# Opening the normed phases of a two-layer streaming encoder with two weight slabs at once

## The reference, cut to what matters

```python
h = rmsnorm(x, norm_mix[0]); proj = h @ l0_w_in          # u, v, z, xbc, dt
ya = gmlp_mix(u, v, ...)
yb = rmsnorm(y_ssd * silu(z), ssm_norm)                  # n_yb
x = x + concat([ya, yb]) @ l0_w_out                      # outa (ya), outb (yb)
for i in (0, 1):
    if i == 1:
        h = rmsnorm(x, norm_mix[1])                      # n_mix1
        x = x + retention_mix(h, ...)                    # heads_a, ret_a, heads_b, ret_b
    h = rmsnorm(x, norm_ffn[i])                          # n_ffn0, n_ffn1
    x = x + (silu(causal_dwconv(h @ w_gate)) * (h @ w_up)) @ w_down   # gu, down
    gate = sigmoid(rmsnorm(x, norm_ple[i]) @ ple_w_gate[i])           # n_ple
    x = x + gate * (p[i] @ ple_w_proj[i])                             # gate, pp
y = rmsnorm(x, norm_final)                               # n_out
```

## The kernel before, in words

| join | last phase | normed phase | norm | slabs after the norm are read by |
|---|---|---|---|---|
| A | z | outb | n_yb | DVE `scaled`, add to x (L1671) |
| B | outb | gu00 | n_ffn0 | gate slab: `scaled`, conv taps (L1697, L1707, L1709 twice), SiLU on ACT, times rstd on POOL (L604); up slab: DVE L1717, L1718 |
| C | gate0 | heads_a | n_mix1 | k and q slab: `scaled`, times cos (L1344), halves swapped by ACT, times sin on POOL (L588), sum (L1347) |
| D | ret_b | gu10 | n_ffn1 | as B |

## Time and profile before

### The profile page before, as it was taken

How to read it: one execution, slowest core, us unless ns; L and a number is a source line. 1 busy time by engine, 2 the same in 40 slices (tenths; PEclk the granted TensorE clock), 3 DMA queues, 4 the chain that set the end, 5 groups by cost and what they waited for, 6 DMA issues and landing times.

```text
span 1856.5 us, 34451 instructions
## 1 busy us (share of the span) xinstructions
PE 1816.7 (98%) x14145; PEld 1768.9 (95%) x14145; DVE 955.9 (51%) x1547; ACT 622.5 (34%) x896; POOL 847.5 (46%) x415
## 2 busy tenths in 40 slices
PE   8999999999999999999899999999999999999996
PEld 7999988999999999999899999999899999999995
DVE  6456777565533542556644441344555415515554
ACT  5334423343221222244433332233334313212342
POOL 4333423466544544565533334333365545544662
PEclk9999999999999999999999999999999999999998
DMA  6222201222342232223222222222122222222221
GB/s 231 79 73 69 80 23 35 74 86 80 114 138 89 81 103 90 74 79 98 80 77 77 77 76 80 88 77 78 54 91 82 89 90 90 91 92 82 66 93 48
DMA packets 49475, 156.80 MB, mean 84 GB/s; under 512 B 5984, under 2 KB 10208, under 8 KB 49376
## 3 DMA queue, kind: packets, MB, share of 16 engines
q1 hardware_dynamic: 43776, 147.67, 24.4%
q10 hardware_dynamic: 5600, 7.74, 1.3%
HBM read 149.75 MB, written 5.63 MB: 84 GB/s over the span
## 4 chain that ended last, share of the span: by engine, by line
PE 90%; DVE 6%; ACT 2%; issue 1%; POOL 0%; DMA 0%; DVEq 0%; POOLq 0%; ACTq 0%
PE proj L318 81%; PE Q L925 6%; DVE arena L1753 1%; ACT arena L622 1%; DVE op_lo L389 1%; DVE arena L1616 0%; DVE arena L1606 0%; ACT op_hi L376 0%; PE Q L1202 0%; DVE rstd L369 0%; DVE x L1755 0%; DVE ssq L1426 0%; PE proj L925 0%; DVE arena L1393 0%; PE Q L329 0%
## 5 line engine op out<-in xcount | busy, mean ns | idle before, releaser
L414 POOL TENSOR_TENSOR w_lo<-w_raw,w_hi 128x1024 fp32r<-128x1024 f32 (+2 forms) x276 | 652.3, 2364 | 760.0 <-ACT w_hi L340 759.7
L318 PE MATMUL proj<-op_hi,w_hi 128*128 128x256 f32 (+1 forms) x4272 | 895.6, 291 | 9.5 <-DVE op_lo L389 5.7
L318 PE MATMUL proj<-op_hi,w_lo 128*128 128x256 f32 (+1 forms) x4272 | 884.6, 288 | 0.0
L318 PE MATMUL proj<-op_lo,w_hi 128*128 128x256 f32 (+1 forms) x4272 | 877.8, 287 | 0.0
L318 PEld LDWEIGHTS proj<-op_hi,w_hi 128*128 128x128 f32 x4272 | 683.5, 189 | 22.6 <-issue 12.3
L318 PEld LDWEIGHTS proj<-op_lo,w_hi 128*128 128x128 f32 x4272 | 686.3, 189 | 0.0
L318 PEld LDWEIGHTS proj<-op_hi,w_lo 128*128 128x128 f32 x4272 | 682.0, 188 | 0.0
L340 ACT ACTIVATE w_hi<-w_raw 128x1024 fp32r<-128x1024 f32 (+2 forms) x276 | 284.8, 1032 | 651.0 <-PE proj L318 650.0
L1393 DVE TENSOR_TENSOR arena<-proj,rstd 128x512 f32<-128x512 f32 (+1 forms) x143 | 98.7, 690 | 220.9 <-PE proj L318 195.4
L1400 DVE TENSOR_TENSOR x<-proj,x 128x512 f32<-128x512 f32 x72 | 49.7, 690 | 223.2 <-PE proj L318 223.2
L622 ACT ACTIVATE arena<-arena 128x32 f32<-128x32 f32 (+5 forms) x217 | 106.0, 514 | 54.6 <-DVE arena L1606 33.2
(11 more groups left out here) (171 smaller groups left out, 1040.2 us busy)
## 6 DMA issues: line engine op xcount, KB each, us to landing
w_raw<-in_w_gu SPq DMA_DIRECT2D x88, 512.0 KB, 3.4
w_raw<-in_w_down SPq DMA_DIRECT2D x32, 512.0 KB, 3.4
w_raw<-in_w_heads_a SPq DMA_DIRECT2D x30, 512.0 KB, 3.4
w_raw<-in_w_heads_b SPq DMA_DIRECT2D x18, 512.0 KB, 3.4
w_raw<-in_w_gate SPq DMA_DIRECT2D x16, 512.0 KB, 3.4
w_raw<-in_w_xbc SPq DMA_DIRECT2D x12, 512.0 KB, 3.3
w_raw<-in_w_down SPq DMA_DIRECT2D x16, 384.0 KB, 3.0
w_raw<-in_w_v SPq DMA_DIRECT2D x8, 512.0 KB, 8.2
```

Of the source, the lines that this page charges most:

```text
L318: last = nc.tensor.matmul(proj[:, 2 * g.mod(2) + half, 0:size], w[:, lo:lo + P], o[:, at:at + size], start=(k == 0 and j == 0), stop=(k == ...
L414: nc.gpsimd.tensor_tensor(w_lo[:, c:c + width], w_raw[:, c:c + width], w_hi[:, c:c + width], ALU.subtract).then_inc(w_lo_done, 1)
```

## The change

PE opens outb, gu00, heads_a and gu10 with `paired`: tiles 0 to 6 of slab 0, then tiles 0 to 6 of slab 1, then tile 7 of both. `mean_square` stands behind 7, 6, 8 and 6 of these tiles (8 means: behind the first tile of slab 1). For the last feature tile (n = 7, `LAST`) ACT squares before it rounds the high half, and in the phases that end in a norm (z, outb, ret_b, gate0, gate1) ACT and POOL do the job of slab 7 before the weight split that stood ahead of it. No operation is added or removed.

```diff
         def act_operand(act, name, n, src):
 
             gain, ops = NORM[name]
+            last = not n.k and n.c == LAST
+            if last:
+                act_square(act, name, n, src)
             nc.scalar.activation(part(op_hi[ops], n, 0, T), src, ACT.Copy, scale=col(gain, n))\
                 .then_inc(nsem("hi"), 1)
-            act_square(act, name, n, src)
+            if not last:
+                act_square(act, name, n, src)
...
-            def phase(name, job=None, per=4):
+            def phase(name, job=None, per=4, late=None):
                 def one(n):
-                    low_ahead(pool, PH[name], n)
+                    last = not n.k and n.c == late
+                    if not last:
+                        low_ahead(pool, PH[name], n)
                     if job:
                         job(n)
+                    if last:
+                        low_ahead(pool, PH[name], n)
...
-            phase("z", lambda n: pool_square(pool, "n_yb", n))
+            phase("z", lambda n: pool_square(pool, "n_yb", n), late=LAST)
```

The ACT side has the same `late` (its `split_ahead` in place of `low_ahead`), and outb, ret_b and gate0/1 get `late=LAST` on both engines. On PE:

```diff
-                def one(n):
-                    slab(pe, ph, n, ops, ready, k0)
-                    if hook and not n.k and n.c == 0:
-                        hook()
-                each(pe, ph.slabs, one, per, peel=4 if hook else 0, least=2)
...
+            def paired(name, ops, norm, k_ms):
+
+                ph = PH[name]
+                ready = (nsem("lo"), ncount(norm, "lo", 1))
+                last = ph.kt - 1
+                early = [(0, k) for k in range(last)] + [(1, k) for k in range(last)]
+                for at, (n, k) in enumerate(early):
+                    if at == k_ms:
+                        mean_square(pe, norm)
+                    slab(pe, ph, At(n), ops, ready if n == 0 else None, ks=range(k, k + 1))
+                for n in range(2):
+                    slab(pe, ph, At(n), ops, ready, ks=range(last, last + 1))
+
+            def normed(name, ops, norm, k_ms):
+
+                paired(name, ops, norm, k_ms)
+                ph = PH[name]
+                each(pe, ph.slabs, lambda n: slab(pe, ph, n, ops) if n.k or n.c >= 2 else None, 4, peel=4, least=2)
...
-            phase("outb", 1, (nsem("lo"), ncount("n_yb", "lo", 1)), hook=norm("n_yb"))
+            normed("outb", 1, "n_yb", 7)
...
-                            slab(pe, PH[name], n + r_, 1, (nsem("lo"), ncount("n_mix1", "lo", 1)) if first and r_ == 0 else None)
                             if first and r_ == 0:
-                                mean_square(pe, "n_mix1")
+                                paired(name, 1, "n_mix1", 8)
+                            elif not (first and r_ == 1):
+                                slab(pe, PH[name], n + r_, 1)
...
-                        phase(f"gu{layer}0", 1 - HID[layer], (nsem("lo"), ncount(LAYER[layer], "lo", 1)), hook=norm(LAYER[layer]))
+                        normed(f"gu{layer}0", 1 - HID[layer], LAYER[layer], 6)
```

More of the change, by code:

```diff
@@ L429, in build @@
         WARM = 8
+        LAST = KD - 1
         V_SCALED = {1: (0, 1, 2), 3: (3, 4, 5), 4: (6, 7)}
@@ L574, in _ @@
             pool_squares(pool, "n_yb", "n_in")
-            phase("z", lambda n: pool_square(pool, "n_yb", n))
+            phase("z", lambda n: pool_square(pool, "n_yb", n), late=LAST)
             pool_squares(pool, "n_ffn0", "n_yb")
-            phase("outb", lambda n: pool_square(pool, "n_ffn0", n))
+            phase("outb", lambda n: pool_square(pool, "n_ffn0", n), late=LAST)
             for layer in range(2):
@@ L591, in _ @@
                     pool_squares(pool, "n_ffn1", "n_mix1")
-                    phase("ret_b", lambda n: pool_square(pool, "n_ffn1", n))
+                    phase("ret_b", lambda n: pool_square(pool, "n_ffn1", n), late=LAST)
                 off = 0
@@ L615, in _ @@
                 pool_squares(pool, nxt, PLE[layer])
-                phase(f"gate{layer}", lambda n: pool_square(pool, nxt, n))
+                phase(f"gate{layer}", lambda n: pool_square(pool, nxt, n), late=LAST)
         @block.scalar
@@ L625, in run, with phase @@
                 return ins
-            def phase(name, job=None, per=4, peel=0):
+            def phase(name, job=None, per=4, peel=0, late=None):
                 def one(n):
-                    split_ahead(act, PH[name], n)
+                    last = not n.k and n.c == late
+                    if not last:
+                        split_ahead(act, PH[name], n)
                     if job:
                         job(n)
+                    if last:
+                        split_ahead(act, PH[name], n)
                 each_ahead(act, PH[name], one, per, peel)
@@ L781, in z_job @@
                 act_operand(act, "n_yb", n, part(xbc, n, 0, T))
-            phase("z", z_job)
+            phase("z", z_job, late=LAST)
             act_root(act, "n_yb")
@@ L787, in outb_job @@
                 act_operand(act, "n_ffn0", n, part(x, n, 0, T))
-            phase("outb", outb_job)
+            phase("outb", outb_job, late=LAST)
             act_root(act, "n_ffn0")
@@ L859, in _ @@
                     heads(act, head, lambda: phase("ret_a"), drain)
-                    phase("ret_b", updated("n_ffn1", PH["ret_b"].g0))
+                    phase("ret_b", updated("n_ffn1", PH["ret_b"].g0), late=LAST)
                     act_root(act, "n_ffn1")
@@ L916, in gate_job @@
                         act_square(act, nxt, n, part(x, n, 0, T))
-                phase(f"gate{layer}", gate_job)
+                phase(f"gate{layer}", gate_job, late=LAST)
                 act_root(act, nxt)
@@ L925, in mm, with phase @@
                 return nc.tensor.matmul(out, w, o, start=start, stop=stop)
-            def phase(name, ops, ready=None, per=4, hook=None, k0=0, start=0):
+            def phase(name, ops, ready=None, per=4, k0=0):
                 ph = PH[name]
-                def one(n):
-                    slab(pe, ph, n, ops, ready, k0)
-                    if hook and not n.k and n.c == 0:
-                        hook()
-                each(pe, ph.slabs, one, per, peel=4 if hook else 0, least=2)
[L937 to L940, removed]
+                each(pe, ph.slabs, lambda n: slab(pe, ph, n, ops, ready, k0), per, least=2)
+            def paired(name, ops, norm, k_ms):
[13 more added lines that the diff above has]
+                each(pe, ph.slabs, lambda n: slab(pe, ph, n, ops) if n.k or n.c >= 2 else None, 4, peel=4, least=2)
             def v_turn(g):
```

## The result

The changed kernel takes 1869.36 us in the median of 4 runs (1868.82 to 1870.34), the kernel before 1858.26 beside it (4 runs): ratio 1.0061, 95% interval 1.0048 to 1.0073, so 11.1 us slower. The direction was right; the time lies outside the range of 1857.5 to 1867.5. The profiled execution took 1870.34 us, its span is 1868.5, and it is 12.1 us behind the one of before.

A forecast was written before the change was run, and what follows sets the result against it. PE, busy 98% of the span, was taken to bound the kernel. The four joins summed to 2.05 us slower, plus 3.4 for one clock fall: 5.45 on the median 1857.77, so 1863.2 us, range 1857.5 to 1867.5.

The forecast's parts named there:

- What costs nothing: Prediction's paragraph pricing at nothing the later last-tile halves (0.64 us), the delayed splits and the loads waiting for them.
- T0: The time when PE starts slab 0 of the normed phase at a join; the forecast counts from it.
- The clock term: Forecast of one fall of the granted clock to half rate, behind the idle at gu10's opening, costing 3.4 us.
- D: The opening of gu10: forecast loss 2.27 us, with PE idle 3.57 before slab 3.
- The rule of the nearest row: Clock falls if a stall is nearer 5.18 us (fell) than 1.39 (stayed), middle 3.3; only gu10's 3.57 exceeds it.
- C: The opening of heads_a: forecast gain 1.83 us, the stall moving from `op_lo` to the squares, 2.95 long.
- B: The opening of gu00: forecast loss 2.62 us, with PE idle 2.93 before slab 3.
- A: The opening of outb: forecast gain 1.01 us, with no wait for the mean.
- the collision: In gu00 and gu10, POOL's split for slab 4 under DVE's conv tap L1709: 2.68 for 0.79, 1.89 us each.
- two falls or three: Rival: the clock also falls at one or both of gu00 and heads_a, 1866.6 or 1870.0 us; chance 0.18.
- a wait of about 3 us: Sign: at heads_a's opening PE waits about 3 us for POOL's ssq.
- L1753's last at 0.73: Sign: POOL's last L1753, in the chain to the squares, takes 0.73 us, where it took 2.70 under the split.

The follow-up runs named there:

- experiment 8: The kernel before, with only the last tile's square put ahead of its rounding in down02 and down12: 1862.29 us against 1858.32, ratio 1.0021.
- experiment 1: The changed kernel, but in down02 and down12 ACT rounds the last tile before squaring it, as before: 1865.72 us against 1857.89, ratio 1.0045.
- experiment 2: The changed kernel with the old square order at n_ple, and gu00 and gu10 opened as before: 1855.75 us against 1857.89, ratio 0.9992.
- experiment 3: The changed kernel with the old square order at n_ple, slab 0's job ahead of slab 4's split in gu00 and gu10: 1857.86 us against 1857.89.
- experiment 4: The changed kernel with the old square order at n_ple and all four joins opened as before, without pairs: 1855.72 us against 1857.89, ratio 0.9990.
- 6: Changed kernel, old n_ple order, gu00 and gu10 unpaired, first head's POOL splits for slabs 4 and 5 behind DVE's sums: 1854.33 us against 1858.32.
- 9: Changed kernel, old n_ple order; outb, gu00, gu10 unpaired, gu means behind 6 tiles; heads_a paired, mean behind 12: 1852.56 us against 1858.63.
- 10: Changed kernel, old n_ple order; outb, gu00, gu10 unpaired; gu/heads_a means behind 6/12 tiles; first-head POOL splits behind sums: 1851.83 us, ratio 0.9966.
- 5: Changed kernel, old n_ple order, gu00 and gu10 opened as before, heads_a paired with the mean behind 12 tiles: 1854.03 us against 1858.32.
- experiment 7: Changed kernel, old n_ple order, first-head POOL splits behind sums, gu00 and gu10 unpaired with the mean behind 6 tiles: 1854.06 us against 1858.32.

## Why the prediction was wrong

The forecast was 5.45 us slower, the measurement 11.1. Of the 5.7 us between them 2.7 are a term that the prediction put at nothing, 2.4 the clock, and about 0.5 the terms that it had.

**The step that failed** stands under "What costs nothing": "The high and low half of the last tile come 0.64 later, but are wanted only at T0 + 11.2." That holds for the four joins. But the edit sits in `act_operand`, which down02 and down12 call as well; the text ahead of the prediction says that the norms n_ple0/1 are left as they are, and they are not. Behind those two phases pp follows, whose operand is not the normed one: there DVE's low half stands in the queue ahead of the copies that free PE's buffer. The high half comes 0.55 late, `op_lo` then meets POOL's add and takes 0.78 more, and PE waits 1.32 longer. That is 1.40 and 1.31 us in the account, and 4.0 us for the edit alone, the clock with it (experiment 8). With the order put back there the time is 1865.72 (experiment 1), inside the range. The prediction looked only where PE waits for the operand, not at what is queued behind it on DVE.

**The clock term was too small.** I gave one fall, at D, 3.4. The profiled execution has three, worth 1.55 (pp0), 1.58 (C) and 2.71 (D), 5.8 together. The rule of the nearest row failed twice: C fell behind 2.96 us, and pp0 behind 1.79, near the 1.39 that had kept its clock, while B's 2.73 kept it. That it came true at D is luck: behind the same gap of 3.29 the clock stayed at 1.00 in experiment 1. The price of one was right at most: 3.4 is the full stretch of 6.8, and two lasted 3.41.

**The terms at full clock** came out near their sizes:

| | forecast | measured |
|---|---|---|
| A | -1.01 | -0.74 |
| B | +2.62 | +2.76 |
| C | -1.83 | -1.86 (experiment 2) |
| D | +2.27 | +2.39 |
| PE idle at B, C, D | 2.93, 2.95, 3.57 | 2.73, 2.96, 3.29 |

Their sum is 2.55 where I had 2.05. With the missed 2.7, the clock's 5.8 and 1.1 that arose ahead of every edit this makes the 12.1. That the collision is what costs at B and D is shown by experiment 3: with POOL's split moved away, pairing costs 0.75 and 0.27 there. At D the size is right and the course is not: the split came 2.50 behind the read, not 1.2, and blocked the second tap instead of the first. The gains at A and C are real, but they aren't the paired opening's, to which the prediction gave them: without any pair A gains 1.21 and C 1.93 (experiment 4). C's stall did move to the squares, and the ropes took part of that back (6).

Of the rivals, "two falls or three" came nearest in what happened (1870.0 for three falls), but its sum lacked the pp term. The signs "no wait for `op_lo` L389", "a wait of about 3 us" and "L1753's last at 0.73" were all there; "a clock window at 0.50 behind D" came with two others, which the prediction had named as a way to be wrong.

**Open:** what decides in which executions the clock falls behind a gap of 2 to 3 us. It is not the length of the gap alone, as the last section shows. And no kernel here has the late splits without the early square, or the square without the splits.

## What to carry to other kernels

Ask of an edit in a shared helper where else it is called, and on each engine what stands queued behind the delayed instruction; the consumer that was meant to wait may not be the one that pays. Finishing two tiles together makes their followers (weight splits, conversions on another engine) start together with the consumer chain, and where two instructions block each other, as POOL's split and DVE's taps do here, the one that starts second waits, even if it is the one on the path. A change made of several parts has to be measured part by part: here the moved splits and the early square made the gains, and the pairs as first placed and the same square at n_ple the losses. An opening is fitted join by join: at C, where the chain to the norm is longer than one slab, a second one helped, but only with the mean behind 12 tiles; at B and D an earlier mean inside the first slab was worth more.

## What was unexpected of the hardware

The same gap of PE came with a fall of the granted clock and without one:

| gap, us | clock fell to 0.50 behind it | clock stayed at 1.00 |
|---|---|---|
| 1.79 | pp0 (changed kernel), pp1 (8) | pp1 (changed kernel), pp0 (8) |
| 2.71 to 2.75 | C (9, 10) | B (changed kernel, 1), C (5) |
| 2.95 to 2.98 | C (changed kernel, 1, 3, 7) | C (2, 6) |
| 3.29 | D (changed kernel) | D (1) |
| 4.29 to 5.19 | C (4, 8, kernel before) | none |

The half-clock stretches behind these gaps lasted 3.41 or 6.83 us; one of 10.24 stands in the SSD part of four of the twelve traces. Gaps of 1.8 to 3.3 us have to be priced as a chance, not a threshold: ten runs of experiment 7 split four to six, 3.0 us apart.
